# Seven block products in place of eight in the downward projection of the inner MLP chunks

## The chip, the cores and the metric

One core of one Trainium2 chip runs the kernel. The metric is device time in microseconds (us) of one execution; for the kernel before three executions were timed. Engines: PE (TensorE), ACT (ScalarE), DVE (VectorE), POOL (GpSimd) and SP (SyncE, which here only issues loads).

## What is computed

A trunk of two layers, each a token mixer (layer 0 a recurrent block, layer 1 sliding-window attention) and an MLP with squared ReLU, a normalisation after each. There are 544 tokens (512 of a prompt, 32 of the sample group), the model is 1024 wide, the MLP's hidden layer 4096. The change touches the two MLPs alone:

```python
def squared_relu_mlp(x, w_up, w_down):
    return jnp.square(jax.nn.relu(x @ w_up)) @ w_down

xp = layer_norm(ALPHA * xp + squared_relu_mlp(xp, mlp_w_up[i], mlp_w_down[i]), ln2_g[i], ln2_b[i])
```

## The kernel before, in words

Every array is kept transposed, features on the 128 partitions and tokens along the row. Tokens are worked in two halves of 256 and 288 columns (`HALF`, `HW` = 288). Each fp32 operand is split into a rounded high part and the rest, `_hi` and `_lo`, and every product is three matmuls: hi by hi, lo by hi, hi by lo. Weights come as pieces of 128x1024 (512 KB) into one of four `stage` buffers; ACT copies a piece into `w_hi` (`split_in`, L681 in the inner chunks, L670 elsewhere), DVE subtracts to get `w_lo` (L1164, L1157). There are eight slots of `w_hi` and `w_lo`. This pair is called a split below.

An MLP runs in eight chunks of 512 hidden features. Chunks 0 and 7 use plain products. In the inner chunks 1 to 6 the upward projection is already done with seven block products instead of eight (the Strassen-Winograd scheme): `chunk_up` on PE runs P1 to P7 by `winograd` (L2258 to L2260), on sums of token blocks that are made once for each MLP (`s1_hi` to `s4_lo`) and on sums of weight blocks. Those weight sums are made by DMAs issued on POOL that add to what is in the buffer (`added`, L1897), five for each chunk, three of them in a buffer of their own, `t1_raw`. ACT takes products out of the PSUM banks (`keep`, L915), DVE adds (`combine`, L1548, L1550) and makes the squared ReLU (L1560, L1599), ACT and DVE split the hidden block into `m_hi` and `m_lo` (L921, L1566).

The downward projection of an inner chunk (`down`, L2232 to L2234 and, through `product`, L2002 to L2004) is plain: for both halves of the tokens and eight output tiles four 128x128 weight tiles each, so 2 x 8 x 4 x 3 = 192 matmuls, half of them 256 and half 288 columns wide. DVE adds each of the 16 results into `acc` (`accumulate`, L1529).

Engines run their instructions in the order written, and semaphores tie them together. Chunks 2 to 5 are one body of a loop that is run four times (`Fori`), the chunks 1 and 6 are written out. SP issues the plain loads, each after a wait on the split that frees its buffer (`load_down`, `load_blocks`, `load_base`). PE uses the eight PSUM banks in turn.

## Time and profile before

| | |
|---|---|
| median of 3 runs | 1091.1 us (1089.22 to 1091.69) |
| the profiled execution | 1089.57 us |
| its span, first to last instruction | 1087.7 us |
| busy PE, DVE, ACT, POOL | 1072.9, 749.5, 564.1, 194.5 us |
| DMA moved | 136.42 MB, 125 GB/s over the span |
| queue of SP and queue of POOL, share of 16 engines | 28.4%, 17.2% |

The profile is of one execution. Busy time of PE is modelled from the starts of its matmuls, which overlap, so the pace of PE is read from the distance of their starts. In a timeline row "x2" stands for two instructions merged, with the time of both together, and what is in brackets is idle time before the row and its releaser.

### The profile page before, as it was taken

What the parts mean: (1) busy time and instruction counts of PE and PEld (TensorE: products, weight loads), DVE (VectorE), ACT (ScalarE), POOL (GpSimd) and SP (SyncE); (2) the same over time, 40 slices, a digit from 0 to 9 for tenths busy, and PEclk for the clock granted to TensorE, in tenths of its full rate; (3) what the DMA queues carried; (4) which work ended last, traced back from release to release, by engine and by line L of the source; (5) the groups of instructions that cost most, each with busy time, mean ns of one, the idle gap of its engine ahead of it and who ended that gap; (6) DMA issues with size and microseconds to landing.
All of it is one profiled execution on the core that took longest, in us unless ns stands there. A gap on an engine that the chain in (4) does not pass through costs nothing.

```text
span 1087.7 us, 22255 instructions
## 1 busy us (share of the span) xinstructions
PE 1072.9 (99%) x8535; PEld 1052.9 (97%) x8535; DVE 749.5 (69%) x1239; ACT 564.1 (52%) x1003; POOL 194.5 (18%) x247
## 2 busy tenths in 40 slices
PE   8999999999999999999999999999999999999996
PEld 8999999999999999999999878999999999999996
DVE  6999999785646657466874664887856556466566
ACT  6999857652432424324666775675432424324233
POOL 2111032001101011012244564300101011010023
PEclk9999999999999999999999999999999999999998
DMA  7323306365848558462141220162858558484202
GB/s 253 113 88 97 111 27 193 60 192 132 216 126 187 169 106 219 111 216 92 27 130 45 77 61 20 59 175 48 229 137 189 172 109 215 126 187 136 78 2 83
DMA packets 53598, 136.42 MB, mean 125 GB/s; under 512 B 5536, under 2 KB 21344, under 8 KB 53504
## 3 DMA queue, kind: packets, MB, share of 16 engines
q1 hardware_dynamic: 44192, 101.10, 28.4%
q0 software_dynamic: 9040, 33.67, 17.2%
q8 instruction: 51, 0.84, 0.3%
q10 hardware_dynamic: 288, 0.59, 0.1%
q14 instruction: 27, 0.22, 0.1%
HBM read 132.81 MB, written 3.56 MB: 125 GB/s over the span
## 4 chain that ended last, share of the span: by engine, by line
PE 92%; DVE 2%; ACT 2%; issue 1%; POOL 1%; DMA 1%; SPq 0%; DVEq 0%; POOLq 0%; ACTq 0%
PE bank L2002 13%; PE bank L2003 13%; PE bank L2004 13%; PE bank L2258 8%; PE bank L2260 8%; PE bank L2259 8%; PE bank L2232 6%; PE bank L2234 6%; PE bank L2233 6%; PE bank L2089 2%; PE bank L2091 2%; PE bank L2090 2%; PE bank L2393 1%; PE bank L2367 1%; PE bank L2411 1%
## 5 line engine op out<-in xcount | busy, mean ns | idle before, releaser
L1164 DVE TENSOR_TENSOR w_lo<-stage,w_hi 128x1024 fp32r<-128x1024 f32 x108 | 130.7, 1221 | 83.5 <-ACT w_hi L681 83.5
L2002 PE MATMUL bank<-x_hi,w_hi 128*128 128x288 f32 (+1 forms) x560 | 163.3, 292 | 2.1 <-DVE w_lo L1157 1.2
L2003 PE MATMUL bank<-m_lo,w_hi 128*128 128x288 f32 (+1 forms) x560 | 162.2, 290 | 0.0
L2003 PE MATMUL bank<-x_lo,w_hi 128*128 128x288 f32 (+1 forms) x560 | 161.7, 289 | 0.0
L2004 PE MATMUL bank<-m_hi,w_lo 128*128 128x288 f32 (+1 forms) x560 | 161.6, 289 | 0.0
L2002 PE MATMUL bank<-m_hi,w_hi 128*128 128x288 f32 (+1 forms) x560 | 161.6, 289 | 0.0
L2004 PE MATMUL bank<-x_hi,w_lo 128*128 128x288 f32 (+1 forms) x560 | 160.9, 287 | 0.0
L681 ACT ACTIVATE w_hi<-stage 128x1024 fp32r<-128x1024 f32 x108 | 110.3, 1053 | 81.3 <-DMA stage<-w_up 61.0
L2232 PE MATMUL bank<-m_hi,w_hi 128*128 128x288 f32 (+1 forms) x512 | 147.7, 288 | 0.3 <-DVE w_lo L1157 0.3
L2234 PE MATMUL bank<-m_hi,w_lo 128*128 128x288 f32 (+1 forms) x512 | 147.6, 288 | 0.0
L2233 PE MATMUL bank<-m_lo,w_hi 128*128 128x288 f32 (+1 forms) x512 | 147.4, 288 | 0.0
L1529 DVE TENSOR_TENSOR acc<-bank,acc 128x288 f32<-128x288 f32 (+1 forms) x196 | 79.8, 439 | 81.3 <-PE bank L2004 65.4
L2258 PE MATMUL bank<-s_hi,w_hi 128*128 128x288 f32 (+1 forms) x384 | 112.4, 293 | 0.0
L2259 PE MATMUL bank<-s_lo,w_hi 128*128 128x288 f32 (+1 forms) x384 | 112.1, 292 | 0.0
L2260 PE MATMUL bank<-s_hi,w_lo 128*128 128x288 f32 (+1 forms) x384 | 111.9, 291 | 0.0
L2002 PEld LDWEIGHTS bank<-x_hi,w_hi 128*128 128x128 f32 x560 | 105.2, 188 | 3.7 <-issue 2.1
L1897 POOL DMA_DIRECT2D t_raw<-w_up x36 | 31.3, 869 | 420.2 <-DMA t_raw<-w_up 352.4
L2002 PEld LDWEIGHTS bank<-m_hi,w_hi 128*128 128x128 f32 x560 | 105.7, 189 | 0.0
L2003 PEld LDWEIGHTS bank<-m_lo,w_hi 128*128 128x128 f32 x560 | 105.5, 188 | 0.0
L2004 PEld LDWEIGHTS bank<-x_hi,w_lo 128*128 128x128 f32 x560 | 105.4, 188 | 0.0
L2003 PEld LDWEIGHTS bank<-x_lo,w_hi 128*128 128x128 f32 x560 | 105.3, 188 | 0.0
L2004 PEld LDWEIGHTS bank<-m_hi,w_lo 128*128 128x128 f32 x560 | 105.3, 188 | 0.0
(283 smaller groups left out, 2798.3 us busy)
## 6 DMA issues: line engine op xcount, KB each, us to landing
stage<-w_up SPq DMA_DIRECT2D x64, 512.0 KB, 5.7
stage<-w_down SPq DMA_DIRECT2D x64, 512.0 KB, 3.7
t_raw<-w_up POOLq DMA_DIRECT2D x36, 512.0 KB, 5.6
stage<-w_up POOLq DMA_DIRECT2D x24, 512.0 KB, 7.8
t_raw<-w_up SPq DMA_DIRECT2D x12, 512.0 KB, 3.6
stage<-w_qkv SPq DMA_DIRECT2D x10, 512.0 KB, 3.9
stage<-w_x SPq DMA_DIRECT2D x8, 512.0 KB, 5.4
stage<-w_y SPq DMA_DIRECT2D x8, 512.0 KB, 3.4
```

The lines of the kernel that those rows point to most:

```text
L681: A(hi, raw, ACT.Copy).then_inc(s_whi, 1)
L1164: vt.tensor_tensor(lo, raw, hi.bitcast(F32), ALU.subtract).then_inc(s_wlo, 1)
L1529: vt.tensor_tensor(a, bank[:, n0 % BANKS, :n], a, ALU.add).then_inc(s_evV, 1)
L2002: mm(out, wh, xh, start=(k == 0), stop=False)
L2003: mm(out, wh, xl, start=False, stop=False)
L2004: ins = mm(out, wl, xh, start=False, stop=(k == last))
L2232: mm(out, wh, xh, start=(k == 0), stop=False)
L2233: mm(out, wh, xl, start=False, stop=False)
L2234: ins = mm(out, wl, xh, start=False, stop=(k == 3))
L2258: mm(out, wh, xh, start=(fresh and k == 0), stop=False, skip_group_check=True)
L2259: mm(out, wh, xl, start=False, stop=False, skip_group_check=True)
L2260: ins = mm(out, wl, xh, start=False, stop=(k == 3), skip_group_check=True)
```

## The change

The downward projection of the inner chunks becomes seven block products too. A chunk's weight block of 512x1024 is cut into 2x2 blocks of 256x512 and the hidden block into 2x2 of 256 features by half of the tokens. The products are D11, DT1, DT2, D22, DT3, D21, DT4, in this order (`down_product`), of 24 matmuls each, over 4 output tiles and 2 tiles of features. Four of them (DT1, DT2, DT3, DT4) are 288 columns wide and three 256.

- Hidden block: H11, H12, H22, and the sums S1, S2, S4, S3 are each split into hi and lo in places of their own (`parts_of`). ACT rectifies (`rectify`), squares twice, once rounded (`square_hi`) and once in fp32 (`square_raw`), or rounds a sum (`part_hi`); DVE makes the four sums (`part_sum`) and seven lo parts (`part_lo`).
- Results: 14 pairs of banks are added into or subtracted from `acc` (`settle`), in place of 16 single adds. DT2, DT3 and DT4, and D22, run on in the banks that D11 and DT1 began, after the pair has been read.
- Weights: 14 splits in a chunk in place of 11. The buffer `t1_raw` is gone. In stage buffer 0 the up chain is worked in place, U11, UT1, UT2, UT4, each made from the last one by an accumulating DMA after its split; in buffer 2 the same for the down chain, D11, DT1, DT2, DT4; buffer 1 takes U22, UT3, D22, DT3 (a load, a sum, a load, a sum); buffer 3 takes U21 and D21. (The first inner chunk's U11 is in buffer 2.) That is six loads on SP and eight accumulating DMAs on POOL in a chunk, before nine and five. The number of bytes is the same.
- The products of the upward projection are the same seven, 168 matmuls, in the order U11, UT1, UT2, U21, UT3, UT4, U22, in banks dealt anew.
- The order of the splits is one table, `AROUND`; ahead of the first inner chunk `FIRST`.
- On the host `w_down` of the inner chunks is stored by blocks.

```diff
+U11, UT1, UT2, U21, UT3, UT4, U22 = UP = tuple(range(7))
+D11, DT1, DT2, D22, DT3, D21, DT4 = DOWN = tuple(range(7, 14))
...
+FIRST = (U11, UT1, U22, UT2, U21, UT3)
+AROUND = ((UT2, 0), (D11, 0), (UT4, 0), (D22, 0), (DT1, 0), (DT2, 0), (U11, 1), (DT3, 0), (DT4, 0), (U22, 1), (D21, 0),
+          (UT1, 1), (U21, 1), (UT3, 1))
+SPLITS = len(AROUND)
...
+        def raw_of(l, c, k):
+
+            st0 = where[job_at[("mlp", l)][0]][0]
+            n = {UT3: 1, U22: 1, D22: 1, DT3: 1, U21: 3, D21: 3, D11: 2, DT1: 2, DT2: 2, DT4: 2}.get(k, 0)
+            if (c, k) == (1, U11):
+                n = 2
+            return stage[:, (st0 + n) % STAGES, :]
...
+            def load_around(l, c, i=0):
+
+                bring(l, c, D21, s_zin, down_block(l, c, 1, 0, i), split_done(l, c, U21, i))
+                bring(l, c, D22, s_yin, down_block(l, c, 1, 1, i), split_done(l, c, UT3, i))
+                if c == CHUNKS - 2:
+                    return
+                bring(l, c + 1, U11, s_xu, up_block(l, c + 1, 0, 0, i), split_done(l, c, UT4, i))
+                bring(l, c + 1, U22, s_yin, up_block(l, c + 1, 1, 1, i), split_done(l, c, DT3, i))
+                bring(l, c + 1, D11, s_xd, down_block(l, c + 1, 0, 0, i), split_done(l, c, DT4, i))
+                bring(l, c + 1, U21, s_zin, up_block(l, c + 1, 1, 0, i), split_done(l, c, D21, i))
...
+                first, last = c == 1, c == CHUNKS - 2
+                low, middle = h11[:, :, 0:256], h12[:, :, :]
+                if not first:
+                    split_in(l, c, UT2, i)
                 for t in range(2):
+                    keep(l, c, i, 0, t, 4, h11[:, t, 0:256])
+                if first:
+                    split_in(l, c, U21)
+                    split_in(l, c, UT3)
                     token_sum(l, 4, s4_hi[:, :, :], raw_b[:, :, 0:256])
+                split_in(l, c, D11, i)
                 for t in range(2):
+                    keep(l, c, i, 2, t, 4, h12[:, t, :], -1.0)
+                if first:
                     act.wait_ge(s_slo, 4 * l + 3)
                     token_sum(l, 3, s3_hi[:, :, :], raw_a[:, :, :])
+                split_in(l, c, UT4, i)
+                split_in(l, c, D22, i)
+                split_in(l, c, DT1, i)
+                keep(l, c, i, 4, 0, 4, h22[:, 0, :], -1.0)
+                rectify(l, c, i, low, 1)
+                square_hi(l, H11, low)
+                keep(l, c, i, 4, 1, 4, h22[:, 1, :], -1.0)
+                square_raw(low)
+                rectify(l, c, i, h22[:, :, :], 2)
+                square_hi(l, H22, h22[:, :, :])
+                square_raw(h22[:, :, :])
+                act.wait_ge(*up_done(l, c, 5, 1, i))
+                b0 = turned(l, 4)
+                A(h21[:, :, :], bank[:, b0:b0 + 2, 0:HW], ACT.Relu).then_inc(s_keep, 1)
+                act.wait_ge(*kept(l, c, 7, i))
+                square_raw(h21[:, :, :])
+                part_hi(l, c, i, S1)
+                split_in(l, c, DT2, i)
+                rectify(l, c, i, middle, 3)
+                square_hi(l, H12, middle)
+                part_hi(l, c, i, S2)
+                square_raw(middle)
+                if not last:
+                    split_in(l, c + 1, U11, i)
+                part_hi(l, c, i, S4)
+                split_in(l, c, DT3, i)
+                part_hi(l, c, i, S3)
+                split_in(l, c, DT4, i)
+                if not last:
+                    split_in(l, c + 1, U22, i)
+                split_in(l, c, D21, i)
+                if not last:
+                    split_in(l, c + 1, UT1, i)
+                    split_in(l, c + 1, U21, i)
+                    split_in(l, c + 1, UT3, i)
...
+            def settle(l, c, i, j, p):
+
+                b0 = turned(l, (0, 4, 0, 4, 0, 4, 0)[j] + 2 * p)
+                m = (0, 4, 4, 4, 4, 0, 0)[j] + 2 * p
+                c0, n = HALF[(0, 1, 0, 0, 1, 0, 1)[j]]
+                a = acc[:, m:m + 2, c0:c0 + n]
+                dve.wait_ge(*pair_done(l, c, j, p, i))
+                if j == 3:
+                    dve.wait_ge(*settled(l, c, 2, p, i))
+                vt.tensor_tensor(a, a, bank[:, b0:b0 + 2, 0:n], ALU.subtract if j in (2, 4) else ALU.add)\
+                    .then_inc(s_acc, 1)
...
+            def chunk_down(l, c, i=0, slabs=lambda k: None):
+
+                last = c == CHUNKS - 2
+                settle(l, c, i, 0, 0)
+                settle(l, c, i, 0, 1)
+                part_lo(l, c, i, S2)
+                part_lo(l, c, i, H12, 4)
+                dve.wait_ge(*summed(l, c, S2, i))
+                part_sum(h12[:, :, :], h12[:, :, :], h22[:, :, 0:256], ALU.add)
+                settle(l, c, i, 1, 0)
+                if not last:
+                    split_in(l, c + 1, U11, i)
+                part_lo(l, c, i, S4)
+                settle(l, c, i, 1, 1)
+                part_sum(h21[:, :, :], h11[:, :, :], h21[:, :, :], ALU.subtract)
+                split_in(l, c, DT3, i)
+                settle(l, c, i, 2, 0)
+                settle(l, c, i, 2, 1)
+                part_lo(l, c, i, S3)
+                split_in(l, c, DT4, i)
+                settle(l, c, i, 3, 0)
+                settle(l, c, i, 3, 1)
+                if not last:
+                    split_in(l, c + 1, U22, i)
+                split_in(l, c, D21, i)
+                slabs(0)
+                settle(l, c, i, 4, 0)
+                settle(l, c, i, 4, 1)
+                slabs(1)
+                if not last:
+                    split_in(l, c + 1, UT1, i)
+                settle(l, c, i, 5, 0)
+                settle(l, c, i, 5, 1)
+                slabs(2)
+                if not last:
+                    split_in(l, c + 1, U21, i)
+                settle(l, c, i, 6, 0)
+                settle(l, c, i, 6, 1)
+                slabs(3)
+                if not last:
+                    split_in(l, c + 1, UT3, i)
...
+                up_sum(l, 1, UT1, 0, 1, s_ux, (s_xu, 16 * (6 * l + 1)))
+                up_sum(l, 1, UT3, 0, 1, s_uy, split_done(l, 1, U22))
+                up_sum(l, 1, UT2, 1, 1, s_ux, split_done(l, 1, UT1))
                 for c in range(1, CHUNKS - 1):
-                    weight_sums(l, c)
+                    up_sum(l, c, UT4, 1, 0, s_ux, split_done(l, c, UT2))
+                    down_sum(l, c, DT1, 0, 1, s_dx, split_done(l, c, D11))
+                    down_sum(l, c, DT3, 0, 1, s_dy, split_done(l, c, D22))
+                    down_sum(l, c, DT2, 1, 1, s_dx, split_done(l, c, DT1))
+                    down_sum(l, c, DT4, 1, 0, s_dx, split_done(l, c, DT2))
+                    if c < CHUNKS - 2:
+                        up_sum(l, c + 1, UT1, 0, 1, s_ux, split_done(l, c + 1, U11))
+                        up_sum(l, c + 1, UT3, 0, 1, s_uy, split_done(l, c + 1, U22))
+                        up_sum(l, c + 1, UT2, 1, 1, s_ux, split_done(l, c + 1, UT1))
 
             def mlp(l):
                 L = 2 * l + 1
...
+            def down_product(l, c, i, k_w, part, b, fresh=False, free=lambda p: ()):
+
+                s = slot_of(l, k_w)
+                xh, xl = parts_of[l][part]
+                pe.wait_ge(*split_done(l, c, k_w, i))
+                pe.wait_ge(*rest_done(l, c, part, i))
+                for m in range(4):
+                    if m % 2 == 0:
+                        for on in free(m // 2):
+                            pe.wait_ge(*on)
+                    out = bank[:, turned(l, b + m), 0:xh.shape[2]]
+                    for k in range(2):
+                        at = 512 * k + 128 * m
+                        wh, wl = w_hi[:, s, at:at + 128], w_lo[:, s, at:at + 128]
+                        mm(out, wh, xh[:, k, :], start=(fresh and k == 0), stop=False, skip_group_check=True)
+                        mm(out, wh, xl[:, k, :], start=False, stop=False, skip_group_check=True)
+                        ins = mm(out, wl, xh[:, k, :], start=False, stop=(k == 1), skip_group_check=True)
+                    if m % 2:
+                        ins.then_inc(s_dn, 1)
+
...
+                def drained(p):
+                    if p == 0:
+                        return combined(l, c, 1, i),
+                    return (read(2), read(3)) if c == 1 else (read(2),)
+
+                def again(j):
+                    return lambda p: (settled(l, c, j, p, i),)
+
+                down_product(l, c, i, D11, H11, 0, True, drained)
+                down_product(l, c, i, DT1, S1, 4, True,
+                             lambda p: (combined(l, c, 3, i) if p else kept(l, c, 7, i),))
+                down_product(l, c, i, DT2, S2, 0, False, again(0))
+                down_product(l, c, i, D22, S4, 4, False, again(1))
+                down_product(l, c, i, DT3, S3, 0, False, again(2))
+                down_product(l, c, i, D21, H12, 4, True, again(3))
+                down_product(l, c, i, DT4, H22, 0, False, again(4))
```

**DVE, the second half of the first inner chunk.** Before (`m_lo` and `h12`, `h21`, `h22` are the hidden block, L1164 a split, L1529 an add into `acc`):

```order
L1560 SCALAR_TENSOR_TENSOR h12_89<-h12_89 128x512
L1164 TENSOR_TENSOR w_lo_50<-stage_51,w_hi_49 128x1024 x2
L1566 TENSOR_TENSOR m_lo_55<-h12_89,m_hi_54 128x2x256
L1599 SCALAR_TENSOR_TENSOR h21_90<-h21_90 128x576
L1560 SCALAR_TENSOR_TENSOR h22_91<-h22_91 128x576
L1566 TENSOR_TENSOR m_lo_55<-h21_90,m_hi_54 128x2x288
L1566 TENSOR_TENSOR m_lo_55<-h22_91,m_hi_54 128x2x288
L1529 TENSOR_TENSOR acc_56<-bank,acc_56 128x256 x4
L1164 TENSOR_TENSOR w_lo_50<-stage_51,w_hi_49 128x1024
```

And of the change, from the fourth sum on (`part_0_5` is S4, `part_0_6` S3; L1279 is a split, L1683 a settled pair, L1672 a sum):

```order
L1672 TENSOR_TENSOR h12_89<-h12_89,h22_91 128x512
L1683 TENSOR_TENSOR acc_56<-acc_56,bank 128x2x288
L1279 TENSOR_TENSOR w_lo_50<-stage_51,w_hi_49 128x1024
L1668 TENSOR_TENSOR part_0_5_lo_113<-h12_89,part_0_5_hi_112 128x512
L1683 TENSOR_TENSOR acc_56<-acc_56,bank 128x2x288
L1672 TENSOR_TENSOR h21_90<-h11_88,h21_90 128x576
L1279 TENSOR_TENSOR w_lo_50<-stage_51,w_hi_49 128x1024
L1683 TENSOR_TENSOR acc_56<-acc_56,bank 128x2x256 x2
L1668 TENSOR_TENSOR part_0_6_lo_115<-h21_90,part_0_6_hi_114 128x576
L1279 TENSOR_TENSOR w_lo_50<-stage_51,w_hi_49 128x1024
L1683 TENSOR_TENSOR acc_56<-acc_56,bank 128x2x256 x2
L1279 TENSOR_TENSOR w_lo_50<-stage_51,w_hi_49 128x1024 x2
```

What was adds between products of PE is now a row of sums, lo parts, pairs and splits that PE's next products take as operands: the first L1279 here is U11 of the next chunk, the next DT3, then DT4, then the "x2" are U22 of the next chunk and D21.

**POOL, accumulating DMAs at the start of an MLP.** Before:

```order
L1897 DMA t1_raw_102<-w_up 128x1024 [waits sum_base_arrived]
L1897 DMA t1_raw_102<-w_up 128x1024 [waits second_sum_added]
L1897 DMA stage_51<-w_up 128x1024 [waits slab_arrived_1]
L1897 DMA stage_51<-w_up 128x1024 [waits slab_lo_done]
L1897 DMA t1_raw_102<-w_up 128x1024 [waits slab_lo_done]
```

And of the change (the first four are UT1, UT3, UT2 and UT4):

```order
L2025 DMA stage_51<-w_up 128x1024 [waits up_chain_base_arrived]
L2025 DMA stage_51<-w_up 128x1024 [waits slab_lo_done] x3
L2025 DMA stage_51<-w_down 128x1024 [waits slab_lo_done] x4
L2025 DMA stage_51<-w_up 128x1024 [waits slab_lo_done] x4
```

Before, the first three waited for arrivals. Now the second (UT3) waits for the split of U22, and the third (UT2), which needs the split of UT1 alone, stands behind it.

**DVE, from chunk 0 to the first inner chunk.** Before:

```order
L1164 TENSOR_TENSOR w_lo_50<-stage_51,w_hi_49 128x1024
L1539 TENSOR_TENSOR acc_56<-bank,acc_56 128x2x288 x3
L1529 TENSOR_TENSOR acc_56<-bank,acc_56 128x288 x2
L1164 TENSOR_TENSOR w_lo_50<-stage_51,w_hi_49 128x1024
L1164 TENSOR_TENSOR w_lo_50<-t1_raw_102,w_hi_49 128x1024
L1164 TENSOR_TENSOR w_lo_50<-stage_51,w_hi_49 128x1024
L1198 TENSOR_TENSOR raw_b_93<-x_hi_52,raw_b_93 128x4x256
L1199 TENSOR_TENSOR raw_b_93<-raw_b_93,x_lo_53 128x4x256
L1204 TENSOR_TENSOR s4_lo_99<-raw_b_93,s4_hi_98 128x1024
```

And of the change (the first "x2" is U11 and UT1, the second U22 and UT2, the third U21 and UT3):

```order
L1279 TENSOR_TENSOR w_lo_50<-stage_51,w_hi_49 128x1024 x2
L1653 TENSOR_TENSOR acc_56<-bank,acc_56 128x2x288 x3
L1643 TENSOR_TENSOR acc_56<-bank,acc_56 128x288 x2
L1279 TENSOR_TENSOR w_lo_50<-stage_51,w_hi_49 128x1024 x2
L1314 TENSOR_TENSOR raw_b_93<-x_hi_52,raw_b_93 128x4x256
L1315 TENSOR_TENSOR raw_b_93<-raw_b_93,x_lo_53 128x4x256
L1279 TENSOR_TENSOR w_lo_50<-stage_51,w_hi_49 128x1024 x2
L1320 TENSOR_TENSOR s4_lo_99<-raw_b_93,s4_hi_98 128x1024
```

The adds of chunk 0's last results stood behind one split and stand behind two; the splits of U22 and UT2 come after the last of them.

## Rows read from the trace of the kernel before

**Rows 1.** Waits of TensorE over the span: engine, line, releaser, total, times, longest
```profile
PE bank L2072 <- DVE w_lo L1157: 2.3, 2, 1.9
```

**Rows 2.** Windows over two inner chunks of layer 0: busy us of each engine
```profile
400.00:445.50 45.50, 45.50 (x362) 45.50 (x361) 26.55 (x38) 16.29 (x22) 4.35 (x5) 1.00 0.63 161
445.50:491.00 45.50, 45.50 (x362) 45.50 (x361) 26.65 (x38) 15.95 (x22) 3.08 (x5) 1.00 0.52 175
```

**Rows 3.** Timeline of PE, start us and us of one matmul
```profile
400.20 0.28 PE L2258 MATMUL bank<-x_hi,w_hi 128*128 128x256 f32 x1
...
405.85 0.30 PE L2258 MATMUL bank<-s_hi,w_hi 128*128 128x288 f32 x1
...
410.65 0.30 PE L2258 MATMUL bank<-s_hi,w_hi 128*128 128x288 f32 x1
```

**Rows 4.** Timeline of DVE in an inner chunk of layer 0
```profile
411.20 0.69 DVE L1566 TENSOR_TENSOR m_lo<-h,m_hi 128x512 fp32r<-128x512 f32 x1 [2.43 <-ACT m_hi L921]
411.81 1.22 DVE L1164 TENSOR_TENSOR w_lo<-t_raw,w_hi 128x1024 fp32r<-128x1024 f32 x1
413.84 2.36 DVE L1164 TENSOR_TENSOR w_lo<-stage,w_hi 128x1024 fp32r<-128x1024 f32 x2 [0.81 <-ACT w_hi L681]
416.12 0.75 DVE L1548 TENSOR_TENSOR h<-h,bank 128x576 f32<-128x576 f32 x1
416.78 1.22 DVE L1164 TENSOR_TENSOR w_lo<-stage,w_hi 128x1024 fp32r<-128x1024 f32 x1
...
422.47 0.76 DVE L1599 SCALAR_TENSOR_TENSOR h<-h 128x576 f32<-128x576 f32 x1 [0.63 <-ACT h L953]
...
427.87 1.22 DVE L1164 TENSOR_TENSOR w_lo<-stage,w_hi 128x1024 fp32r<-128x1024 f32 x1
```

**Rows 5.** Timeline of ACT in the same chunk, with what it waited for
```profile
410.48 0.62 ACT L921 ACTIVATE m_hi<-h 128x512 fp32r<-128x512 f32 x1
411.00 0.40 ACT L915 ACTIVATE h<-bank 128x288 f32<-128x288 f32 x1
...
412.76 3.89 ACT L681 ACTIVATE w_hi<-stage 128x1024 fp32r<-128x1024 f32 x4
...
423.33 1.36 ACT L921 ACTIVATE m_hi<-h 128x576 fp32r<-128x576 f32 x2 [0.96 <-DVE h L1599]
...
431.54 1.06 ACT L681 ACTIVATE w_hi<-t_raw 128x1024 fp32r<-128x1024 f32 x1 [4.35 <-DMA t_raw<-w_up]
437.51 1.06 ACT L681 ACTIVATE w_hi<-stage 128x1024 fp32r<-128x1024 f32 x1 [4.91 <-DMA stage<-w_up]
```

**Rows 6.** Timeline of POOL in the same chunk: issues of accumulating transfers
```profile
416.86 0.87 POOL L1897 DMA_DIRECT2D t_raw<-w_up  x1 [26.49 <-DMA t_raw<-w_up]
426.06 0.87 POOL L1897 DMA_DIRECT2D t_raw<-w_up  x1 [8.34 <-DMA t_raw<-w_up]
426.60 1.22 POOL L1897 DMA_DIRECT2D stage<-w_up  x1
429.38 0.86 POOL L1897 DMA_DIRECT2D stage<-w_up  x1 [1.55 <-DVE w_lo L1164]
```

**Rows 7.** Timeline of SP in the same chunk: plain loads, first issue to last
```profile
415.10 6.51 SPq L520 DMA_DIRECT2D stage<-w_up  x4
```

**Rows 8.** DMA issues by kind: KB each, median us to landing
```profile
stage<-w_down SPq DMA_DIRECT2D x64, 512.0 KB, 3.7
```

**Rows 9.** First and last start of the first products' matmuls (line L2258)
```profile
L2258 PE MATMUL bank<-x_hi,w_hi x288: 280/282/298, 218.3 to 1001.3; 128*128 128x256 f32 x96, 128*128 128x288 f32 x48
```

**Rows 10.** Timeline of DVE at the first inner chunk of layer 0
```profile
218.84 1.21 DVE L1164 TENSOR_TENSOR w_lo<-stage,w_hi 128x1024 fp32r<-128x1024 f32 x1
...
222.24 1.22 DVE L1198 TENSOR_TENSOR raw_b<-x_hi,raw_b 128x1024 f32<-128x1024 f32 x1
```

**Rows 11.** Windows near the end: granted clock is the sixth figure, after five engines' busy
```profile
1078.00:1079.00 1.00, 0.00 (x1) 0.00 (x0) 0.62 (x4) 0.20 (x1) 0.00 (x0) 1.00 0.00 0
...
1080.00:1081.00 1.00, 0.98 (x5) 0.73 (x4) 0.66 (x1) 0.00 (x0) 0.00 (x0) 0.50 0.00 0
```

589 lines of the change are left out of this document (263 added, 326 removed).

## Prediction

> **What bounds the kernel now.** I read the page's busy times first: PE 1072.9 us of the span's 1087.7, DVE 749.5, ACT 564.1. Then PE's waits: the longest line over the whole span is 2.3 us [rows 1], so PE sets the time. Then the windows over two inner chunks: 45.5 us each, PE busy all of it, DVE 26.6, ACT 16 [rows 2]. Then the pace of PE, by starts and not by durations, since matmuls overlap: 48 matmuls of 256 columns from 400.20 to 405.85, 0.1177 us each, and 36 of 288 columns from 405.85 to 410.65, 0.1333 us each [rows 3]. An inner chunk is 96 wide and 72 narrow matmuls up, 96 and 96 down: 192 x 0.1333 + 168 x 0.1177 = 45.4 us, as the windows say. So whatever is taken off PE is gained, as long as PE still never waits.
>
> **Taken off PE.** The downward products fall from 192 to 168 matmuls (96 wide, 72 narrow): 24 x 0.1177 = 2.8 us less in each of 12 inner chunks, 33.9 us in all. An inner chunk is 42.5 us of PE work. With no wait the profiled 1089.6 us would be 1055.7.
>
> **What DVE gets.** Paces, start to start: a split 1.13 us, an item of 576 elements 0.66, one of 512 elements 0.61 [rows 4]; ACT 0.95 for a split (four in 3.89) and 0.52 for 512 elements, so some 0.58 for 576, an estimate between these [rows 5]. A hand-over costs 0.1 us from DVE to ACT (422.47 + 0.76 to 423.33) and 0.29 from DVE to POOL (427.87 + 1.22 to 429.38) [rows 4 to 6]. DVE's chunk is now 14 splits (15.8), 14 pairs of which 8 narrow (8.8), 7 lo parts (4.5), 4 sums (2.6) and 3 combines (1.9): 33.6 us. That fits into 42.5. The order does not fit, and here I laid one chunk out, engine by engine, in the written order. New is that PE's downward operands are made from results of the same chunk, one after another, by ACT and DVE.
>
> Chain one, from the end of UT4 (time 0). ACT takes the product out, squares it, DVE makes S1, ACT rounds it: four items and their hand-overs, 3.2 us; ACT is still at H22 and comes 0.8 late, so 4.0. From there DVE has in order, without a gap: S1's lo, combine, sum S2, split DT2, two pairs, S2's lo, H12's lo, sum S4, pair, split U11, S4's lo, pair, sum S3, split DT3, two pairs, S3's lo, split DT4, two pairs, split U22, split D21. That is 6 splits, 7 items of 576 and 10 of 512: 6.8 + 4.6 + 6.1 = 17.5. The last is an operand of D21, so D21 starts at 21.6. PE reaches it after U22, D11, DT1, DT2, D22, DT3: 3 x 2.8 + 3 x 3.2 = 18.1. So PE waits 3.5 us in each chunk for DVE alone, some 2.1 of it already ahead of DT3, for S3's lo, and small ones ahead of DT2 and D22.
>
> Chain two. U22 of the next chunk stands ahead of D21 in both ACT's and DVE's order, and its load waits for the split of DT3, which ends at 15 (4.0 and 11.0 us of the row above). A plain load alone takes 3.7 us [rows 8]; here it shares the engines with the sum for UT1, and an accumulating transfer that ran beside four plain loads took 9.2 us (416.86 to 426.06) where the next took 5.5 (to ACT's 431.54) [rows 5 to 7]. So I take 4.5 for the load, landed at 19.6, then ACT 0.95, DVE 1.13 for U22 and 1.13 for D21, and hand-overs: 23.1. PE's wait grows from 3.5 to 5.1.
>
> Chain three. ACT splits DT1 ahead of taking out UT3's first tile, and UT4 needs that bank. DT1's sum is issued 1.5 us behind UT4's, and sums in one queue land 3.0 apart: those issued from 426.06 on, three of them, have the first landed at 431.54 and the third at 437.51 [rows 5, 6]. DT1 lands 14.3 into the chunk, and PE waits 0.5 ahead of UT4.
>
> A chunk of the loop is then 42.5 + 5.1 + 0.5 = 48.2 against 45.5: **2.7 more, 8 times, 21.6.**
>
> **The first inner chunk.** It starts at 218.3 on PE [rows 9], and DVE gets to its next split at 218.84, after the last add of chunk 0 [rows 10]. Now that split is U22, ended at 220.06; POOL issues UT3's sum at 220.35 and only then UT2's, though UT1's split was long done. The first lands after 5.5, the second 3.0 later, 228.9; ACT and DVE split it until 231.2. PE wants UT2 at 218.3 + 2.8 + 3.2 = 224.3 and waits 7.1 us (rounding included). ACT stands at that split too, with U21 and UT3 behind it, and DVE then has the two token adds of 1.22 each [rows 10]: 2.5 us ahead of U21 and UT3, and 3.6 instead of 0.5 ahead of UT4. With 5.1 as above it is 42.5 + 18.3 = 60.8, **15.3 more, twice, 30.6.**
>
> **The last inner chunk and the seam to chunk 7.** Without U11 and U22 of a next chunk the waits are some 2.1, so 44.7, 0.8 less than before. But the fourth slab of chunk 7 is loaded after D21's split and split by DVE after the last pair, where four slabs were done between the adds before: load, ACT, DVE end 2.4 us after PE is free. **1.6 more, twice, 3.2.**
>
> **At nothing.** ACT's added squares, rounds and splits: from 16 to some 27 us of a chunk, hidden except where a chain names them. Bytes are the same, six loads and eight sums. Past the MLPs nothing is moved.
>
> Sum: 1089.6 + 21.6 + 30.6 + 3.2 = **1145.0 us**. The profiled execution is 1.5 below the median, within the runs' spread, and I leave it so. A difference of 0.2% (2.2 us) is about what a measurement can tell from none.
>
> What the trace does not show is an accumulating transfer in this company. Lower bound of its price: a plain load's 3.7 us [rows 8]. Upper: 9.2 [rows 6]. I take 5.5 alone and 3.0 apart, the row that is nearest, since it too was followed by other sums.
>
> **The rivals.**
>
> *Light DMA.* Sums cost what plain loads do, 3.7 and some 1.6 apart. Then chains two and three vanish and chain one is left: 42.5 + 3.5 = 46.0, 0.5 x 8 = 4; in the first chunk UT2 comes 3.2 earlier, so 42.5 + 3.9 + 2.5 + 3.5 = 52.4, 6.9 more, twice; the seams 3. 1089.6 + 4 + 14 + 3 = 1111. For it: the DMA share in the two windows is 0.63 and 0.52 [rows 2], so there is room. Against: the 3.0 us spacing. Chance 0.25. The Trainium skill, DMA: Bandwidth & Descriptors, section Anatomy of one DMA — SWDGE (gpsimd) path, gives about 2.0 us plus the bytes at 436 GB/s, an estimate of 3.2 us for these 512 KB and 1.2 apart, which would make it about 1109. The trace has 5.5 and 3.0 for sums, so it disagrees.
>
> *Heavy DMA.* Sums 3.5 apart and loads 0.2 longer, on the way to the 9.2 seen. The up chain's splits then come late as well: waits ahead of UT2 1.3, UT4 1.9 and D21 0.8 more, a loop chunk of 51.9. 1089.6 + 6.4 x 8 + 2 x 21.5 (first chunk 17.8 more and the seam with its chunk some 4) = 1184. Chance 0.10.
>
> *Clock.* The granted clock stayed at 1.00 through PE's idle stretch 1078 to 1079 and was 0.50, the lower level of 1.2 GHz, at 1080 [rows 11]. If each wait ahead of D21 does the same, a product behind it costs double, some 3.0 more: 12 x 3.0 = 36, 1181. If only the 7.1 us wait does, 6, 1151. Chance 0.08. The skill's TensorE: Matmul & The Clock Gate, section HAM oscillation — how this bites in real kernels, tells of just this, a tile that starts cold after each DMA wait; no stretch inside an MLP here shows it yet.
>
> *Faster.* DVE's row is the mechanism: it decides from 3.5 us on. If ACT and DVE get from UT4's end to D21's split in under 18.1 us, because items overlap more than their paces in the old order show, PE never waits in the loop, and the 33.9 stand against the first chunk's UT2 and U21 (7.1 + 2.5) and the seam (2.4), both twice: 1089.6 - 33.9 + 19.2 + 4.8 = 1079.7. For it: DVE is only 79% loaded. Against: 17.5 us of its items are counted one by one. Chance 0.09.
>
> That PE's work does not shrink can't be: the new order has 168 downward matmuls in a chunk.
>
> **Numbers.** Forecast 0.45 (its own range 1128 to 1162), light 0.25, heavy 0.10, clock 0.08, faster 0.09, and 0.03 that parts cancel to within 0.2%. Slower by over 0.2% holds 0.88. The range takes in light and heavy with some room below, 1098 to 1184, and leaves out faster and the far ends.
>
> **What would show it.** In the changed profile: waits of PE of about 7 us at a product of the first inner chunk, released by DVE's split, twice; in each loop chunk one of about 3 us ahead of D21 released by a split and one of about 1.5 ahead of DT3 released by a lo part; inner chunks 48 us apart; sums landing 5.5 after issue when alone; clock 1.00. It would be wrong if PE's idle time in the inner chunks were under 3 us, or DVE idled while PE waits.

## The result, and the profile after

The changed kernel takes **1165.0 us** (median of 4 runs, 1163.2 to 1167.7), the kernel before 1090.2 in the same session: ratio 1.069, interval 1.066 to 1.071. Forecast was 1145.0 with a range of 1098 to 1184, so the sign and the range hold, and 20 us are missing from the forecast.

Busy times and DMA queues of the changed kernel, from the page (queue: packets, MB, share of 16 engines' span; last two rows: KB each, median us from issue to landing):

```profile
PE 1074.9 (92%) x8247; PEld 1043.0 (89%) x8247; DVE 846.4 (73%) x1289; ACT 669.8 (57%) x1159; POOL 225.3 (19%) x283
...
q0 software_dynamic: 14224, 52.55, 25.7%
q1 hardware_dynamic: 39296, 83.28, 21.8%
...
stage<-w_up SPq DMA_DIRECT2D x54, 512.0 KB, 4.1
...
stage<-w_up POOLq DMA_DIRECT2D x48, 512.0 KB, 5.6
stage<-w_down POOLq DMA_DIRECT2D x48, 512.0 KB, 6.5
```

PE has fewer matmuls, but it is busy 92% of the span and not 99%. Its waits, where before the longest line was 2.3 us and none lay in an inner chunk [rows 1]:

```profile
PE bank L2412 <- DVE w_lo L1279: 21.4, 10, 2.6
PE bank L2412 <- DVE part_lo L1668: 16.9, 19, 1.7
PE bank L2393 <- DVE w_lo L1279: 15.5, 3, 7.6
PE bank L2393 <- ACT h L1007: 10.7, 8, 3.5
```

L2412 is a down product, L2393 an up product. The 21.4 are the waits ahead of D21, some 2.1 each; 16.9 those ahead of DT3, DT2 and D22; 15.5 are two waits of 7.6 ahead of UT2 in the first inner chunks; 10.7 those ahead of UT4, for ACT's read of UT3's tile. Single waits in the text below are read from the distance of PE's starts, less one matmul, and come out 0.15 to 0.2 us longer than in these lines.

The starts of PE's matmuls give the length of each inner chunk, seam to the next included. Against 45.5 before [rows 2]: first inner chunk 63.1 us (layer 0) and 64.6 (layer 1), loop chunks 46.9 to 51.7 with a mean of 49.5, last 50.1 and 46.7. The twelve take 620.3, where they took 546. The difference, 74.3, is all but 4 us of what the profiled execution lost (1167.7 against 1089.6). Windows over the first inner chunk, three loop chunks of layer 0 and one of layer 1 (columns as in [rows 2]; the last three are granted clock, DMA share and GB/s):

```profile
218.00:281.20 63.20, 49.04 (x339) 48.01 (x338) 39.63 (x46) 27.85 (x38) 8.63 (x10) 0.86 0.63 132
332.00:380.60 48.60, 43.67 (x337) 42.78 (x337) 33.71 (x42) 23.38 (x35) 6.91 (x8) 1.00 0.67 145
380.60:431.80 51.20, 45.66 (x339) 44.42 (x337) 35.62 (x43) 26.77 (x37) 6.91 (x8) 0.97 0.70 149
431.80:479.00 47.20, 43.76 (x339) 42.87 (x338) 33.66 (x42) 23.60 (x34) 6.91 (x8) 1.00 0.69 150
953.10:1004.70 51.60, 46.98 (x338) 45.85 (x337) 35.60 (x43) 26.69 (x37) 6.88 (x8) 0.93 0.69 146
```

DVE went from 26.6 to about 34 us a chunk, as counted (33.6). Two things stand out: the clock is below 1.00 in some chunks, and those with it at 1.00 are the short ones: three loop chunks without a low stretch take 46.9 to 48.7 us, five with one 49.1 to 51.7. That suggests that the clock is the missing 20 us. It is the first theory to be tested, and it is wrong.

The first inner chunk, on POOL, ACT, DVE and PE:

```profile
220.14 1.75 POOL L2025 DMA_DIRECT2D stage<-w_up  x2 [37.06 <-DVE w_lo L1279]
```
```profile
229.42 1.06 ACT L774 ACTIVATE w_hi<-stage 128x1024 fp32r<-128x1024 f32 x1 [17.15 <-DMA stage<-w_up]
```
```profile
218.62 1.21 DVE L1279 TENSOR_TENSOR w_lo<-stage,w_hi 128x1024 fp32r<-128x1024 f32 x1
230.51 1.23 DVE L1279 TENSOR_TENSOR w_lo<-stage,w_hi 128x1024 fp32r<-128x1024 f32 x1 [10.67 <-ACT w_hi L774]
```
```profile
223.94 0.29 PE L2395 MATMUL bank<-s_hi,w_lo 128*128 128x288 f32 x1
231.83 0.58 PE L2393 MATMUL bank<-s_hi,w_hi 128*128 128x288 f32 x1 [7.60 <-DVE w_lo L1279]
232.21 0.44 PE L2394 MATMUL bank<-s_lo,w_hi 128*128 128x288 f32 x1
232.45 0.44 PE L2395 MATMUL bank<-s_hi,w_lo 128*128 128x288 f32 x1
```

DVE ends U22's split at 219.8, POOL issues UT3's and UT2's sums together, UT2's is there at 229.4, and UT2 starts 7.8 late. Its matmuls are then 0.24 us apart instead of 0.133: the clock had fallen during the wait (0.50 from 228 us on).

### The profile page after: what moved, and what is told of

Same layout as the page of the kernel before. It is cut to its first block, busy times and chain, and to the rows that moved or that the text cites. A ratio compares the mean times of both kernels' runs of the same rounds, so it can differ in the third digit from the quotient of the medians.

```text
span 1165.9 us, 21579 instructions
## 1 busy us (share of the span) xinstructions
PE 1074.9 (92%) x8247; PEld 1043.0 (89%) x8247; DVE 846.4 (73%) x1289; ACT 669.8 (57%) x1159; POOL 225.3 (19%) x283
## 3 DMA queue, kind: packets, MB, share of 16 engines
q0 software_dynamic: 14224, 52.55, 25.7%
## 4 chain that ended last, share of the span: by engine, by line
PE 43%; DMA 22%; DVE 17%; issue 8%; ACT 7%; POOL 1%; SPq 0%; DVEq 0%; ACTq 0%; POOLq 0%
DMA stage<-w_up 13%; DMA stage<-w_down 8%; PE bank L2136 8%; PE bank L2137 8%; PE bank L2138 8%; DVE w_lo L1279 7%; ACT w_hi L774 4%; DVE acc L1683 3%; PE bank L2223 2%; PE bank L2225 2%; PE bank L2224 2%; DVE h L1672 2%; DVE part_lo L1668 1%; PE bank L2532 1%; DVE w_lo L1273 1%
## 5 line engine op out<-in xcount | busy, mean ns | idle before, releaser
L1279 DVE TENSOR_TENSOR w_lo<-stage,w_hi 128x1024 fp32r<-128x1024 f32 x168 | 202.6, 1220 | 134.4 <-ACT w_hi L774 134.0
L2412 PE MATMUL bank<-part_hi,w_hi 128*128 128x288 f32 (+1 forms) x672 | 204.1, 304 | 42.0 <-DVE w_lo L1279 21.4
L2414 PE MATMUL bank<-part_hi,w_lo 128*128 128x288 f32 (+1 forms) x672 | 200.3, 298 | 0.0
L2413 PE MATMUL bank<-part_lo,w_hi 128*128 128x288 f32 (+1 forms) x672 | 200.1, 298 | 0.0
L2412 PEld LDWEIGHTS bank<-part_hi,w_hi 128*128 128x128 f32 x672 | 132.9, 198 | 50.4 <-issue 28.1
L2414 PEld LDWEIGHTS bank<-part_hi,w_lo 128*128 128x128 f32 x672 | 133.2, 198 | 0.0
L2413 PEld LDWEIGHTS bank<-part_lo,w_hi 128*128 128x128 f32 x672 | 133.2, 198 | 0.0
L2393 PE MATMUL bank<-s_hi,w_hi 128*128 128x288 f32 (+1 forms) x384 | 114.6, 299 | 16.1 <-DVE w_lo L1279 15.5
L1683 DVE TENSOR_TENSOR acc<-acc,bank 128x512 f32<-128x512 f32 (+1 forms) x168 | 113.9, 707 | 11.6 <-PE bank L2414 11.5
L2393 PE MATMUL bank<-x_hi,w_hi 128*128 128x256 f32 (+1 forms) x288 | 85.1, 296 | 10.7 <-ACT h L1007 10.7
L2393 PEld LDWEIGHTS bank<-s_hi,w_hi 128*128 128x128 f32 x384 | 74.0, 193 | 17.1 <-issue 16.2
L1273 DVE TENSOR_TENSOR w_lo<-stage,w_hi 128x1024 fp32r<-128x1024 f32 x66 | 80.0, 1230 | 10.5 <-ACT w_hi L768 10.4
```

The source lines that it names most:

```text
L1279: vt.tensor_tensor(w_lo[:, s, :], raw_of(l, c, k), w_hi[:, s, :].bitcast(F32), ALU.subtract)\
L1683: vt.tensor_tensor(a, a, bank[:, b0:b0 + 2, 0:n], ALU.subtract if j in (2, 4) else ALU.add)\
L2393: mm(out, wh, xh[:, k, :], start=(fresh and k == 0), stop=False, skip_group_check=True)
L2412: mm(out, wh, xh[:, k, :], start=(fresh and k == 0), stop=False, skip_group_check=True)
L2413: mm(out, wh, xl[:, k, :], start=False, stop=False, skip_group_check=True)
L2414: ins = mm(out, wl, xh[:, k, :], start=False, stop=(k == 1), skip_group_check=True)
```

## The experiments

Theories: **order** (the forecast's: PE waits where an operand's sum or split stands too late in a queue), **clock** (PE runs at half pace after its waits), **sums** (accumulating transfers are too slow for where they stand). Times against the kernel before, on the same chip in each group. The table has the inner chunks, us, read from the starts on PE:

| kernel | median us | ratio, 95% interval | first, layer 0 / 1 | mean of 8 loop chunks | last with seam | twelve |
|---|---|---|---|---|---|---|
| before | 1090 | | 45.5 / 45.5 | 45.5 | 45.5 / 45.5 | 546 |
| changed | 1165.0 | 1.066 to 1.071 | 63.1 / 64.6 | 49.5 | 50.1 / 46.7 | 620.3 |
| e1_first_queue | 1159.6 | 1.061 to 1.066 | 54.0 / 55.7 | 50.3 | 49.7 / 48.7 | 610.4 |
| e2_d21_early | 1143.2 | 1.047 to 1.051 | 58.3 / 59.7 | 47.3 | 49.9 / 47.8 | 594.3 |
| e3_u11_late | 1168.2 | 1.070 to 1.076 | 57.6 / 59.4 | 50.2 | 51.9 / 49.2 | 619.7 |
| e4_dt2_keep | 1160.6 | 1.064 to 1.070 | 60.6 / 61.8 | 49.3 | 48.2 / 47.1 | 612.2 |
| e5_three | 1114.0 | 1.020 to 1.023 | 48.5 / 49.2 | 46.5 | 49.5 / 47.1 | 566.4 |
| e6_no_add | 1128.2 | 1.031 to 1.041 | 54.5 / 54.2 | 47.3 | 46.6 / 45.4 | 579.2 |
| e7_filler | 1171.7 | 1.074 to 1.078 | 62.6 / 58.8 | 49.7 | 49.9 / 51.2 | 620.6 |
| e8_d22_early | 1106.6 | 1.013 to 1.016 | 49.0 / 50.1 | 45.6 | 46.4 / 47.6 | 557.4 |
| e9_best | 1115.7 | 1.022 to 1.029 | 47.6 / 46.8 | 46.7 | 47.7 / 47.7 | 563.8 |
| e10_no_add_filler | 1121.7 | 1.029 to 1.032 | 54.7 / 54.8 | 46.1 | 47.0 / 47.0 | 572.5 |
| e11_best_no_add | 1086.4 | 0.995 to 0.998 | 44.7 / 44.6 | 44.1 | 45.9 / 45.9 | 534.1 |
| e12_ring | 1132.7 | 1.037 to 1.040 | 48.0 / 48.5 | 48.8 | 49.5 / 50.5 | 587.0 |

### Is it the clock?

```diff
+                for _ in range(n):
+                    mm(out, x_hi[:, 1, 0:128], x_hi[:, 0, 0:256], start=True, stop=True, skip_group_check=True)
...
+                    keep_busy(l, 64, 2)
                 up_product(l, c, i, UT2,
...
+                keep_busy(l, 18, 4)
                 down_product(l, c, i, D21,
```

(The first line stands in a helper, `keep_busy`; 26 more matmuls stand ahead of UT4 in the first chunk.)

> The changed kernel, with matmuls of 256 columns into an idle bank on PE, whose results nobody reads, issued just ahead of its longest waits: 64 ahead of UT2 (7.5 us for a wait of 7.8) and 26 ahead of UT4 (3.1 for 3.5) in the first inner chunk, and 18 ahead of D21 (2.1 for 2.1 to 2.8) in every inner chunk. It prices the clock alone, since nothing comes sooner. Clock theory (the stretches of granted clock 0.50 behind these waits are what stands between the forecast of 1145 and the measured 1165): the low stretches of the inner chunks go, and the time falls by about 25 us, to 1138 to 1145. Rival, PE's low clock lies beside waits that another engine sets, so that a faster PE only waits longer: 1160 to 1170.

Measured 1171.7, and in the profiled execution the twelve chunks take 620.6 us where they took 620.3. Windows over the first inner chunk and two of the loop:

```profile
218.40:281.10 62.70, 57.36 (x447) 55.95 (x446) 39.55 (x46) 27.05 (x38) 8.64 (x10) 1.00 0.61 129
380.20:430.30 50.10, 46.36 (x357) 45.11 (x356) 34.61 (x42) 25.30 (x36) 6.91 (x8) 1.00 0.68 146
430.30:480.00 49.70, 46.42 (x355) 45.05 (x355) 34.61 (x42) 24.98 (x36) 6.91 (x8) 1.00 0.70 149
```

The clock is 1.00 throughout and the loop chunks take 49.7. The low stretches had cost nothing in sum: with PE at full pace its waits in a loop chunk, the filled one included, are 6.4 us where they were 5.2. The idle matmuls did not hold D21 back where it had a wait: in ten chunks it starts 0.05 to 0.13 us after its split ends, with them as without. In the two last chunks, which had none, it starts 2.0 later. The first chunk of layer 1 did shrink, 64.6 to 58.8; 4.5 of that went in the last chunk of the same layer. So the clock theory falls, though the low clock and the long chunks do go together.

### Is it the sums?

```diff
-                pt.dma_start(dst, src, accum_op=ALU.add).then_inc(done, 16)
+                pt.dma_start(dst, src).then_inc(done, 16)
```

> The sums on POOL's queue are plain copies of the second block: the same queue, bytes and order, without the adding (the products then run on wrong weights, so the output is not the reference's). If the adding is what makes a sum slow (5.5 us alone, 3.0 behind another): landings fall to 4 us and 1.6, the waits ahead of UT2 in the first chunks from 7.8 to 4, those ahead of DT2 and UT4 in the loop go: about 1140 us. If the queue on POOL costs it (descriptors made by software) and not the adding: landings and time stay, 1160 to 1168.

Measured 1128.2: 37 us less. Its rows for the queue and the landings:

```profile
q1 hardware_dynamic: 39296, 83.28, 23.2%
q0 software_dynamic: 14224, 52.55, 14.7%
...
stage<-w_up POOLq DMA_DIRECT2D x48, 512.0 KB, 3.9
stage<-w_down POOLq DMA_DIRECT2D x48, 512.0 KB, 4.6
```

The same queue, packets and bytes: 14.7% of 1128.7 us is 166 us of all 16 engines, where the sums took 25.7% of 1165.9, 300 us. It is the adding that costs, 1.8 times the engine time and 1.7 to 1.9 us more to landing. The Trainium skill, DMA: Bandwidth & Descriptors, section Anatomy of one DMA — SWDGE (gpsimd) path, gives 2.0 us plus the bytes at 436 GB/s, an estimate of 3.2 us for 512 KB. That lies 0.7 and 1.4 below these plain copies (3.9 and 4.6) and 2.4 and 3.3 below the sums (5.6 and 6.5): for a sum the measured row decides.

In the loop only two waits are left in e6, 1.3 ahead of DT3 and 2.0 ahead of D21: the waits ahead of UT2, UT4, DT2 and D22 came with the sums. And now the loop chunks are of two kinds, by clock:

```profile
320.80:368.50 47.70, 44.68 (x338) 44.26 (x337) 34.73 (x43) 25.49 (x36) 4.22 (x8) 0.96 0.50 154
828.10:874.10 46.00, 43.12 (x337) 42.70 (x337) 34.08 (x43) 25.11 (x35) 4.23 (x8) 1.00 0.49 161
```

### The clock once the sums are quick

The two edits together, with fewer idle matmuls.

> e6_no_add with the idle matmuls ahead of the waits that it has: 32 ahead of UT2 and 10 ahead of UT4 in the first chunk, 16 (1.9 us) ahead of D21 in every inner chunk. Again the sums only copy and the output is not the reference's. In e6 8 loop chunks were of two kinds: 47.7 us with 3.4 us of granted clock 0.50 in them (6), and 46.1 without (2). If the low clock costs time once sums are not late, all are 46.1 to 46.3 and the time falls by 6 x 1.6 + about 2 = 11 us to 1117. If it costs nothing here either (as in e7_filler against the changed kernel): 1126 to 1130.

Measured 1121.7. All eight loop chunks take 46.0 to 46.4:

```profile
320.60:366.90 46.30, 45.15 (x354) 44.76 (x353) 34.46 (x43) 25.52 (x36) 4.23 (x8) 1.00 0.50 158
```

So a low stretch costs 1.6 us here, where PE and DVE set the pace, and nothing where the sums do. The loop gives 9.3 us; 2 us go back in the last chunks, which had no wait ahead of D21 to fill, and 0.8 in the first. By the medians alone e6 and e10 can hardly be told apart (their intervals touch); the loop chunks do it. The four kernels (changed, e6, e7, e10) are one table of two by two: sums slow, 1165 and 1172; sums quick, 1128 and 1122.

### One edit of order each

```diff
-                up_sum(l, 1, UT3, 0, 1, s_uy, split_done(l, 1, U22))
                 up_sum(l, 1, UT2, 1, 1, s_ux, split_done(l, 1, UT1))
+                up_sum(l, 1, UT3, 0, 1, s_uy, split_done(l, 1, U22))
```

> Only the order of two sums in POOL's queue at the start of each MLP is turned: UT2's before UT3's. Queue theory (UT2's sum stands behind UT3's, which waits for the split of U22): in the first inner chunk PE's waits of 7.8 us ahead of UT2 and 3.5 to 3.7 ahead of UT4 go, 11 us of waiting an MLP, 22 in all, and with them most of the 17 us of granted clock 0.50 there, 5 to 6 us more an MLP: 1165 - 22 - 11 = 1132 us. If the low clock costs nothing of its own: 1143. Rival, the backlog of DVE and ACT (chunk 0's last adds and the token adds) is what is late: UT4's wait stays and part of UT2's, 1150 or more.

Measured 1159.6. The cause of UT2's wait is shown: its 7.8 us are gone and the first chunk 9 us shorter in both layers. The price is not: UT3 now waits 1.5, UT4 still 2.8 and 4.2 (the rival's part), and in this execution the loop chunks are 0.8 longer each. Of 18 us 8 came back within the same MLPs.

```diff
                 part_lo(l, c, i, S3)
+                split_in(l, c, D21, i)
                 split_in(l, c, DT4, i)
...
                     split_in(l, c + 1, U22, i)
-                split_in(l, c, D21, i)
```

> D21's split stands right behind S3's lo part on DVE (behind S3's rounding on ACT), ahead of the splits of DT4 and of the next chunk's U22. Order theory (D21 waits only because its split is written last): the waits of 2.1 to 2.8 us ahead of D21 go in 10 chunks, 23 us, the seams to chunk 7 get 1 to 2 shorter, and the stretches of granted clock 0.50 that begin behind these waits go too, some 1.7 us each for 5 of them: 1165 - 23 - 8 - 3 = 1131 us. The waits of 1.4 ahead of DT3 stay. Rival, DVE as a whole is late at that point: the wait moves on to DT4 and the time stays within 5 us of 1165.

Measured 1143.2, 22 us less. The group of waits "L2412 <- DVE w_lo" (21.4 us) has left the list of waits; ahead of DT3 1.3 stays, ahead of DT2 it is 0.8 to 2.2 now. The 11 us expected of clock and seam did not come: one loop chunk still has a low stretch, where five had, yet a loop chunk is shorter only by the 2.2 that D21's wait had been; the seam stayed at 4.2 in layer 0.

```diff
                 split_in(l, c, D21, i)
+                if not last:
+                    split_in(l, c + 1, U11, i)
                 split_in(l, c, DT4, i)
```

(and U11's split is taken out between the two adds of DT1.)

> As the run before, and the split of the next chunk's U11 moves from between two adds behind D21's split, so that S4's lo, S3's sum, DT3's split and S3's lo come 1.1 us sooner on DVE. Chain theory (DVE's items from S1's rounding to S3's lo set DT3): the waits ahead of DT3 fall from 1.4 to some 0.3 and those of 0.3 ahead of D22 go, 1.3 x 10 = 13 us below the run before, about 1118. Rival, the sum for UT1 is issued 5 us later and now lands late: waits of 1 to 3 us ahead of UT1 or UT2 of the next chunk, and the time is at or above that of the run before.

Measured 1168.2, 25 above e2: the rival. The wait ahead of DT3 fell from 1.3 to 0.8, and there are new ones. Waits of PE in one loop chunk of e3:

```profile
PE bank L2412 <- DVE part_lo L1668: 2.3, 2, 1.6
PE bank L2393 <- DVE w_lo L1279: 1.6, 1, 1.6
PE bank L2393 <- DVE acc L1683: 1.2, 1, 1.2
```

UT1's sum comes late, DVE stands at UT1's split, and D21's adds stand behind that, whose banks U11 needs. 1.1 us won in one line cost 3 in another.

```diff
+                    down_sum(l, c, DT2, 1, 1, s_dx, split_done(l, c, DT1))
                     down_sum(l, c, DT3, 0, 1, s_dy, split_done(l, c, D22))
-                    down_sum(l, c, DT2, 1, 1, s_dx, split_done(l, c, DT1))
```

(and ACT reads UT3's first tile ahead of DT1's split.)

> In POOL's queue DT2's sum is issued ahead of DT3's, and ACT takes UT3's first tile out ahead of DT1's split, nothing else. Landing theory (a sum behind another lands 3 us later): the waits ahead of DT2 (0.3 to 1.9 us, 8.7 in all) and those ahead of UT4 in the loop (0.4 to 1.5 us, 4.8 in all) go, and perhaps one or two stretches of low clock: 1150 to 1153 us. The 3.5 us ahead of UT4 in the first chunks falls little. Rival, DT3's sum now lands 3 us later and its split with it: the wait ahead of DT3 grows from 1.4 to 2 or 3 and eats the gain, 1165 or above. Rival, DVE is late at DT2 anyway: 1160.

Measured 1160.6. The waits ahead of DT2 fell to 0.2 and those ahead of UT4 went, but D21's grew to as much as 2.9 and UT4's second tile now waits, up to 2.7 in the first chunks and 0.7 to 1.5 in five others. Together the 4 to 5 us of the weakest reading.

### Together

The three edits of e1, e2 and e4 in one kernel.

> The edits of e1_first_queue, e2_d21_early and e4_dt2_keep together. Each alone gave 5, 22 and 4 us. Additive theory (each wait is its own): 1165 - 31 = 1134 us. Joint theory (what one edit took away came back as another wait or as low clock in the next chunks, because the chain of operands stayed late somewhere): with all three the loop chunk has only some 0.3 ahead of D22, 1.3 ahead of DT3 and 0.3 ahead of UT2 left, 44.5 us, the first chunk 47, the last 44.5 and a seam of 4.0 and 2.3: 8 x 44.6 + 2 x 47 + 2 x 44.5 + 6.3 = 546 us for the twelve, where the changed kernel has 620.5 of 1165.9: about 1091 us, level with the kernel before.

Measured 1114.0: 51 us, where the three alone gave 31. Neither theory met it. The loop speaks for the joint one in kind: a chunk changed by +0.8, -2.2 and -0.2 us with each alone, and by -3.0 with all three. (e1 alters nothing in a loop chunk, so its +0.8 came from the chunks before or from this one execution; without it the sum is -2.4.) The first chunks changed by 9, 5 and 3, and by 15 together, so there they are nearly each its own. Left in the loop are 1.4 ahead of DT3, 0.3 ahead of D22, up to 1.2 ahead of UT2, and 0.5 to 1.7 ahead of UT4's second tile, which the expectation had left out:

```profile
PE bank L2393 <- ACT h L1007: 10.3, 12, 2.0
```

Then, instead of e4's turn on POOL, DVE's order (ACT's alike):

```diff
-                split_in(l, c, UT4, i)
                 split_in(l, c, D22, i)
+                split_in(l, c, UT4, i)
...
+                split_in(l, c, DT3, i)
                 split_in(l, c, DT2, i)
...
                 part_sum(h21[:, :, :], h11[:, :, :], h21[:, :, :], ALU.subtract)
-                split_in(l, c, DT3, i)
```

> e1_first_queue and e2_d21_early, ACT's read of UT3's first tile ahead of DT1's split, and new: D22's split stands ahead of UT4's (so the sum for DT3 is issued some 4 us sooner and DT2's has none ahead of it), DT3's split stands ahead of DT2's on ACT and DVE, where DVE idles for DT2's sum (1.4 us), and the five transfers for the cache on POOL's queue wait until chunk 7's slabs are split. DVE then has one split less between S1 and S3's lo. Chain theory: the waits ahead of DT2, D22 and DT3 go but for 0.3 or so, a loop chunk takes 43 to 44 us, the first 46, the last 43.5 and both seams 2.3: about 535 us for the twelve, 1080 in all, faster than the kernel before by 10. Rival: D22's load is issued only after UT3's split and now comes late for ACT, which stands there with UT4's split behind it: waits of 1 to 3 us ahead of UT4, 1095 to 1110.

Measured 1106.6, the best kernel that computes everything. Loop chunks are 45.1 to 46.4 and both seams 2.2, but DT2's wait stayed at 1.3: DT3's split, put ahead of DT2's, took the place of the idle time and pushed S2's lo part back. The time is in the rival's range, but not by its cause: UT4 waits 0.3 to 0.5 in three loop chunks, not 1 to 3 in each. Windows of a loop chunk of e8 and, below, of the kernel e11 further down:

```profile
407.00:452.10 45.10, 43.72 (x339) 42.90 (x338) 34.60 (x43) 25.07 (x35) 6.91 (x8) 1.00 0.76 162
```
```profile
353.00:397.10 44.10, 43.21 (x338) 42.74 (x337) 34.66 (x43) 24.84 (x35) 4.22 (x8) 1.00 0.52 166
```

```diff
+                combine(l, c, i, 6, 6, h12[:, :, :], 4)
                 part_lo(l, c, i, S1)
-                combine(l, c, i, 6, 6, h12[:, :, :], 4)
...
                 settle(l, c, i, 2, 0)
-                settle(l, c, i, 2, 1)
                 part_lo(l, c, i, S3)
+                settle(l, c, i, 2, 1)
+                if not last:
+                    split_in(l, c + 1, U11, i)
```

> e8_d22_early and four more moves. DVE: the combine of U22's product stands ahead of S1's lo, where DVE idles 0.75 us for ACT; S3's lo stands between DT2's two adds; the next chunk's U11 is split behind them. SP: U21's load ahead of D11's. First chunk: DVE splits U22 ahead of chunk 0's last adds, so that UT3's sum is issued some 6 us sooner. Chain theory (what is left in a loop chunk of 45.4 us is DVE's written order between S1 and S3's lo, 1.3 us ahead of DT2, 0.3 D22, 0.2 DT3): a loop chunk falls to 44.3, the first from 49.5 to 47, the last by 1: 557 - 8 x 1.1 - 2 x 2.5 - 2 = 541 for the twelve, 1090 in all, level with the kernel before. Rival, as with e3: U11's split 4 us later makes the sum for UT1 late and PE waits ahead of U11, UT1 or UT2: 1107 or above.

Measured 1115.7: the rival again. DT2 waits 0.7, DT3 and D22 nothing, but UT2 waits 1.3 to 2.2 in every loop chunk for its sum. The line of these waits, which e11 below does not have:

```profile
PE bank L2393 <- DVE w_lo L1279: 15.3, 11, 2.0
```

e9 and the edit of e6 together:

> e9_best with plain copies in place of the sums; output again not the reference's. If sums no longer bind in that order, it is within 3 us of e9_best. If they still do, it is 5 to 15 us below it. The twelve inner chunks cannot be under 12 x 42.5 = 510 us, 1056 in all, if PE's work is what was counted.

Measured 1086.4, 29 below e9, more than either reading. The same order as e9, and no wait ahead of UT2 at all; the eight loop chunks are alike to 0.2 us. What stands between e9 and e11 is only whether the transfers add.

The last one moves UT2's sum and splits ahead of UT3's:

```diff
                 if not last:
+                    split_in(l, c + 1, UT1, i)
+                settle(l, c, i, 4, 0)
...
                     split_in(l, c + 1, U21, i)
                 settle(l, c, i, 6, 0)
+                slabs(3)
                 settle(l, c, i, 6, 1)
-                slabs(3)
                 if not last:
-                    split_in(l, c + 1, UT3, i)
+                    split_in(l, c + 1, UT2, i)
```

> e9_best with U11's split back between the adds (as in e8_d22_early), so that UT1's sum is not late, and three moves around the end of a chunk: UT1's split ahead of the adds of DT3's product, UT2's sum and splits ahead of UT3's (UT3's split goes behind D11's in the next chunk), and in the last inner chunk chunk 7's fourth slab is split between the last two adds instead of behind them. Queue theory (in e9_best PE's wait of 1.3 to 2.2 us ahead of UT2 is UT2's sum, issued behind UT3's and after a late U11): that wait goes, 0.7 is left ahead of DT2 and 0.3 ahead of D22, a loop chunk takes 44.4 us, the seam 1 instead of 2.5: 8 x 44.4 + 2 x 47 + 2 x 45.5 = 540 for the twelve, some 1089 in all, within 3 us of the kernel before. Rival: the sums are simply too slow for one ring of four buffers, the wait moves on to UT3 or D22 (whose load now starts later), and the time stays at 1100 to 1107.

Measured 1132.7: the rival, and worse than it said. UT2's wait is gone and one of 2.6 to 3.9 ahead of UT4 is there. ACT in a loop chunk of e12:

```profile
419.62 1.06 ACT L774 ACTIVATE w_hi<-stage 128x1024 fp32r<-128x1024 f32 x1 [0.49 <-DMA stage<-w_up]
...
429.00 2.00 ACT L774 ACTIVATE w_hi<-stage 128x1024 fp32r<-128x1024 f32 x2 [4.58 <-DMA stage<-w_down]
```

UT3's split is now at 419.6; D22's load takes UT3's buffer, lands at 429.0, and UT4's split stands behind it on ACT.

### What the 50 us are

In the changed kernel the issue of UT4's sum comes at 337.31, 386.62, 436.93 and 484.56: 49.3, 50.3 and 47.6 apart; in e7 at 387.36 and 437.00, 49.6 apart with PE busy for longer. One turn, on POOL, ACT, DVE and SP of the changed kernel:

```profile
386.62 0.86 POOL L2025 DMA_DIRECT2D stage<-w_up  x1 [8.68 <-DVE w_lo L1279]
...
396.48 0.87 POOL L2025 DMA_DIRECT2D stage<-w_down  x1 [7.51 <-DVE w_lo L1279]
398.22 0.87 POOL L2025 DMA_DIRECT2D stage<-w_down  x1 [0.87 <-DVE w_lo L1279]
...
426.76 0.86 POOL L2025 DMA_DIRECT2D stage<-w_up  x1 [2.73 <-DVE w_lo L1279]
```
```profile
392.74 2.01 ACT L774 ACTIVATE w_hi<-stage 128x1024 fp32r<-128x1024 f32 x2 [2.31 <-DMA stage<-w_up]
395.32 1.06 ACT L774 ACTIVATE w_hi<-stage 128x1024 fp32r<-128x1024 f32 x1 [0.57 <-DMA stage<-w_down]
...
406.39 1.06 ACT L774 ACTIVATE w_hi<-stage 128x1024 fp32r<-128x1024 f32 x1 [2.41 <-DMA stage<-w_down]
...
429.77 2.01 ACT L774 ACTIVATE w_hi<-stage 128x1024 fp32r<-128x1024 f32 x2 [6.27 <-DMA stage<-w_up]
434.32 1.06 ACT L774 ACTIVATE w_hi<-stage 128x1024 fp32r<-128x1024 f32 x1 [2.54 <-DMA stage<-w_up]
```
```profile
407.49 1.23 DVE L1279 TENSOR_TENSOR w_lo<-stage,w_hi 128x1024 fp32r<-128x1024 f32 x1 [1.44 <-ACT w_hi L774]
...
421.64 2.36 DVE L1279 TENSOR_TENSOR w_lo<-stage,w_hi 128x1024 fp32r<-128x1024 f32 x2 [0.80 <-ACT w_hi L774]
```
```profile
395.23 21.95 SPq L644 DMA_DIRECT2D stage<-w_up  x2
...
424.18 0.33 SPq L644 DMA_DIRECT2D stage<-w_up  x1
```

UT4's sum is issued at 386.6 and split from 392.7, and DT1's split follows. DT2's sum, issued at 398.2 behind DT3's, is there at 406.4, 8.2 later. Then DVE works through its row to D21's split, ended at 424.0. That frees U21's buffer, whose load of 424.2 is there at 429.8, with UT3's sum beside it. UT2's sum, issued at 426.8 behind UT3's, is there only at 434.3, 7.6 later, after ACT has split U21 and UT3. Then UT2 is split, and the next UT4's sum can go at 436.9. No step in this turn waits for PE. That the sums hold the chunk up and that the clock does not is shown by e6 and e7. That it is this ring, link by link, is read from one turn and only argued. Its period is not fixed either: the loop chunks of this one execution are 46.9 to 51.7 us apart, and why they differ is open.

## Why the prediction was right or wrong

- **PE's work, 42.5 us a chunk: right to 0.4.** In e6 a last inner chunk reaches its seam after 43.1 us with no wait over 0.3 in it. In e11 a loop chunk is 44.1, of which 1.2 are waits.
- **Chain one, 3.5 us of waiting for DVE's row: right in kind, a little high.** Where the sums are quick (e6) it is 1.3 ahead of DT3 and 2.0 ahead of D21, 3.3 together; I had put 2.1 of it ahead of DT3. But 0.6 to 0.8 of it is DVE idle for U22's load, which is chain two, so DVE's row alone is worth about 2.6, an estimate from these. The row itself, without its idle times, is 17.7 us for 17.5; it begins 3.1 us after UT4 in e6's loop and 3.1 to 3.9 after it in the changed kernel's, not 4.0. e2 took D21's part away.
- **Chain two, 1.6 more: the link was there at 1.0, and one of 0.9 was missed.** U22's load took 3.7 (issued at 416.9, landed at 420.55), not the 4.5 that I took, and DVE idles 0.8 to 1.5 for it in the loop chunks, 1.0 on average. I had DVE without a gap from S1 on. It idles up to 1.7, 0.9 on average, for DT2's sum, which lands 8.2 us after its issue, behind DT3's in the queue: waits of up to 1.9 ahead of DT2. I had costed this queueing at UT2 in the first chunk and not here. The page of the kernel before warned of it. The forecast's 5.5 is near what its 36 sums into `t1_raw` took (5.6); its sums into `stage` took more:

```profile
stage<-w_up POOLq DMA_DIRECT2D x24, 512.0 KB, 7.8
```

- **Chain three, 0.5 ahead of UT4: right,** 0.4 on average.
- **The waits of a loop chunk, 5.6: right at 5.2, and yet the chunk is 49.5 and not 48.2.** The sum of the waits came out right partly by luck, since chain one was too high by some 0.9 and DVE's idle time for DT2's sum was not in it at all. This is the step that failed: I made a chunk from PE's work plus its waits, with the transfers at fixed distances and the clock at 1.00, and did not follow the sums and buffers once around. Read on PE, the missing 1.3 is the low clock (42.9 of work, 5.2 of waits, 1.3 of half pace). e7 shows that it is not its cause: at clock 1.00 the loop chunk is 49.7 and the waits are longer instead. The turn of the sums and buffers, read once at 50.3 us, would explain that; it is argued, not shown. Eight chunks, 1.3 each, are some 10 of the 20; with the two items below that makes 19, and the rest lies outside the inner chunks.
- **The first inner chunk, 60.8: a little low,** at 63.1 and 64.6. UT2's wait was 7.8 for 7.1 (the forecast's own terms give 6.9), by the cause given (e1); UT4's 3.5 and 3.7 for 3.6; the 2.5 ahead of U21 and UT3 was only 0.2 and 0.6; the waits sum to 15.0 in layer 0, not 18.3, and PE at half pace behind UT2's makes up more than the difference. 6 of the 20.
- **The last chunk and seam, 94.2 for both layers: low by 2.6.** The seam in layer 0 was 3.9 and in layer 1 2.2; the transfers for the cache on POOL's queue run beside chunk 7's slabs in layer 0 alone, and with them moved behind (e8) it is 2.2 in both.
- **Rivals.** Light: tested by e6 at 1128, not 1111; the difference is mostly low clock (1.6 in six loop chunks) and 54 instead of 52 in the first. Its premise, a sum that costs a copy, does not hold. Clock: its mechanism came (drops behind waits of 2.1 to 2.8 ahead of D21 in some chunks), its price did not. Its chance of 0.08 as a separate case was a poor question, since its cost depends on what else binds. Heavy: the slowest kind of sum has a median of 6.5 us to landing, and the one followed here took 8.2, not 9.2. Faster: DVE's row was as long as counted.
- **The signs named beforehand.** One sign of being wrong came: DVE idles while PE waits, 10.67 us ahead of UT2's split in the first chunk. The forecast's own account of that wait implies this, so the sign was badly chosen. The clock of 1.00 did not come; PE's waits of 7 and 2 us and sums at 5.6 did.

Of the 75 us lost, the edits of order in e8 give back 58. Plain copies give back 37 in the order of the change and 29 in that of e9, so the two causes overlap. No order tried here beats the kernel before; the best is 1.5% behind it, and even e11, whose sums do not add, is only 0.2 to 0.5% ahead. What remains in e8 is 3.5 to 5 in each first chunk, 1 to 2 at each seam, a loop chunk level with before (24 matmuls saved, and spent on waiting), and some 6 us outside the inner chunks, which were not looked into.

## What to carry to other kernels

Taking work off the bound engine pays only as far as the rest can go round faster. Before costing a change by the bound engine's work plus its waits, follow each buffer once around (load, sum, split, use, load) and add up the turn: if it is longer than the engine's, the turn is the better forecast. (Here that was seen only afterwards; no forecast was made by it.) And before a low clock is blamed, keep the engine busy through its waits: if the time stays, another ring sets the pace.

## What the runs showed of the hardware

A transfer of 512 KB that adds into its target used 1.8 times the DMA engines' time of a plain copy by the same queue, and landed 1.7 to 1.9 us later (5.6 and 6.5 for 3.9 and 4.6). The byte count of a sum is thus no measure of its load.

The granted clock fell behind some waits ahead of D21 and not behind others of the same length. Windows at two of them in the changed kernel (first figure after the span: PE busy; sixth: granted clock):

```profile
274.00:276.00 2.00, 2.00 (x12) 2.00 (x12) 1.95 (x4) 0.00 (x0) 0.00 (x0) 0.53 0.97 135
```
```profile
373.00:375.00 2.00, 0.55 (x4) 0.56 (x5) 2.00 (x4) 0.82 (x1) 0.86 (x1) 1.00 0.00 0
375.00:377.00 2.00, 2.00 (x19) 2.00 (x18) 2.00 (x3) 0.00 (x0) 0.00 (x0) 1.00 0.90 145
```

After 2.3 us of waiting PE ran at 0.53 in one, the lower level of 1.2 GHz for nearly all of the window, and after 2.2 us at 1.00 in the other. What tells the two apart the runs do not show.
